# Features of the second half in two of three units, constants loaded first, samples four and first joins five steps later

## What is computed

```python
h = rmsnorm(x, norm_gain) * (1 + scale) + shift          # features: 1024 per token
qa, ka, va, za, qb, fb, ib, zb, ga, gb = split(h @ w_in)   # projections
# branch A: three head groups, windows 128 keys back at distance 1, 4, 16
s = q @ k.T * scale - slope * dist;  m = max(s);  p = exp(s - m);  l = sum(p)
o, lse = p @ v / l, m + log(l)                            # prompt; the sample also reads a cache of keys and values
o_a = sum_g softmax_g(lse_g) * o_g                         # join of the three groups
A = (o_a * silu(za)) @ w_branch_a
B = (rmsnorm(hgrn2(silu(qb), sigmoid(fb), ib)) * silu(zb)) @ w_branch_b
y = x + gate * ((sigmoid(ga) * A + sigmoid(gb) * B) @ w_out)
```

## Time and profile before

| | us |
|---|---|
| median of 3 runs (3123.8 to 3127.46) | 3126.55 |
| the profiled execution: its time | 3124.32 |
| its span, first to last instruction | 3122.5 |
| PE busy of the span | 2919.9 |
| projections, recurrence (`phase_weave`) | about 110 to 2121 |
| attention (`phase_mix`) | about 2121 to 2719 |

### The profile page before, as it was taken

The page is one execution under the profiler, slowest core; times in us unless marked ns, Lnnn a source line. Parts: engine busy times, 40 slices in busy tenths (PEclk is TensorE's granted clock), DMA queues, the critical chain, the costliest instruction groups (busy, mean ns, idle before and its releaser), DMA issues. The chain is left out here.

```text
span 3122.5 us, 47274 instructions
## 1 busy us (share of the span) xinstructions
PE 2919.9 (94%) x18020; PEld 2609.9 (84%) x18020; DVE 1361.6 (44%) x3061; ACT 1085.1 (35%) x2165; POOL 836.7 (27%) x704
## 2 busy tenths in 40 slices
PE   7889999999999899999999999995979889589999
PEld 7778998888888799999999999993656656389999
DVE  2584334566544233343565645422434334433333
ACT  1343213444444333212444444442534434221110
POOL 0242333555422222232555533210011112040000
PEclk9999999999999999999999999997989797799999
DMA  6364432332322432322333232227676776353432
GB/s 195 95 178 137 125 95 77 105 98 92 104 99 88 166 113 94 111 84 88 95 100 102 90 100 94 98 71 263 240 262 224 254 246 212 123 194 109 126 119 86
DMA packets 385264, 417.90 MB, mean 134 GB/s; under 512 B 115600, under 2 KB 296080, under 8 KB 378384
## 3 DMA queue, kind: packets, MB, share of 16 engines
q1 hardware_dynamic: 378128, 406.24, 41.0%
q10 hardware_dynamic: 6912, 8.65, 0.8%
HBM read 284.11 MB, written 130.70 MB: 133 GB/s over the span
## 5 line engine op out<-in xcount | busy, mean ns | idle before, releaser
L667 PE MATMUL weave_bank<-h_high,w_high 128*128 128x352 f32 (+2 forms) x2240 | 819.8, 366 | 15.2 <-issue 11.4
L669 PE MATMUL weave_bank<-h_high,w_low 128*128 128x352 f32 (+2 forms) x2240 | 801.4, 358 | 0.0
L668 PE MATMUL weave_bank<-h_low,w_high 128*128 128x352 f32 (+2 forms) x2240 | 799.1, 357 | 0.0
L944 POOL TENSOR_TENSOR w_low<-weave_w_raw,w_high 128x512 fp32r<-128x512 f32 x284 | 379.9, 1349 | 771.1 <-ACT w_high L815 769.2
L667 PEld LDWEIGHTS weave_bank<-h_high,w_high 128*128 128x128 f32 x2240 | 427.0, 191 | 57.5 <-issue 14.7
L669 PEld LDWEIGHTS weave_bank<-h_high,w_low 128*128 128x128 f32 x2240 | 426.0, 190 | 40.4
L668 PEld LDWEIGHTS weave_bank<-h_low,w_high 128*128 128x128 f32 x2240 | 426.0, 190 | 39.7 <-issue 2.9
L679 PE MATMUL weave_bank<-w_high,h_high 128*128 128x256 f32 x1088 | 310.0, 285 | 0.0
L681 PE MATMUL weave_bank<-w_high,h_low 128*128 128x256 f32 x1088 | 306.7, 282 | 0.0
L680 PE MATMUL weave_bank<-w_low,h_high 128*128 128x256 f32 x1088 | 305.6, 281 | 0.0
L1671 ACT ACTIVATE mix_probs<-mix_scores,mix_o_out 128x256 f32<-128x256 f32 (+1 forms) x384 | 157.0, 454 | 319.2 <-DVE mix_o_out L1754 307.1
(11 more groups left out here) (229 smaller groups left out, 4860.6 us busy)
## 6 DMA issues: line engine op xcount, KB each, us to landing
weave_w_raw<-in_w_qkv SPq DMA_DIRECT2D x144, 256.0 KB, 2.9
mix_kv<-in_kT_c SPq DMA_DIRECT2D x24, 1024.0 KB, 7.6
mix_kv<-in_v_c SPq DMA_DIRECT2D x24, 1024.0 KB, 7.1
tail_gates<-scratch_gates SPq DMA_DIRECT2D x48, 352.0 KB, 3.2
weave_w_raw<-in_w_g SPq DMA_DIRECT2D x64, 256.0 KB, 3.0
weave_w_raw<-in_w_b SPq DMA_DIRECT2D x60, 256.0 KB, 2.8
scratch_sums<-mix_o_out SPq DMA_DIRECT2D x48, 264.0 KB, 6.0
mix_rows<-scratch_sums SPq DMA_DIRECT2D x24, 528.0 KB, 6.8
```

The lines of the kernel that those rows point to most:

```text
L667: pe.matmul(dst, w_high[:, i, k, :], h_high[:, k, tok], start=(k == 0), stop=False)
L668: pe.matmul(dst, w_high[:, i, k, :], h_low[:, k, tok], start=False, stop=False)
L669: mm = pe.matmul(dst, w_low[:, i, k, :], h_high[:, k, tok], start=False, stop=(k == KD - 1))
L944: pool.tensor_tensor(w_part(w_low, p), w_raw[p % RAW][:, :, :], w_part(w_high, p), ALU.subtract).then_inc(w_low_done, 1)
```

## The change

It moves work and adds none.

1. Chunk f of the features starts in unit 2 + 3f // 2 (units 2, 3, 5, 6, 8, 9, ..., 26) and keeps its distances between stages.
2. SP issues the seven constants of the projections first, then x and weight pieces in turn.
3. All parts of the sample in the attention, with their loads, `prepare` and copies, come four steps later (`at` begins with 8 instead of 4).
4. The first half of each join but the last pair's is weighed and turned five steps later (`later`); its `rows` are still loaded in the step `start`.

```diff
+        F_AT = {2 + 3 * f // 2: f for f in range(FT)}
...
-                for p in range(4, 7):
-                    load(p)
-                for f in range(FX):
-                    load_x(f)
                 for dst, src in CONSTANTS:
                     sp.dma_start(dst, dr[src]).then_inc(const_in, 16)
+                load_x(0)
+                load(4)
+                load_x(1)
+                load(5)
+                load(6)
+                for f in range(2, FX):
+                    load_x(f)
                 for U in range(len(STEPS)):
...
-                    if 1 <= U < FT + 1:
-                        feature_sums(U - 1)
+                    if U - 1 in F_AT:
+                        feature_sums(F_AT[U - 1])
...
-                    if 1 <= U < FT + 1:
-                        feature_pairs(U - 1)
-                    if 3 <= U < FT + 3:
-                        feature(U - 3)
+                    if U - 1 in F_AT:
+                        feature_pairs(F_AT[U - 1])
+                    if U - 3 in F_AT:
+                        feature(F_AT[U - 3])
...
-    at = lambda i, k: 4 + SPAN * i + k * SPAN // PARTS
+    at = lambda i, k: 8 + SPAN * i + k * SPAN // PARTS
...
-    turn_at = lambda jp, half: start(jp, half) + (12 if jp < PAIRS - 1 else 6 + 2 * half)
+    later = lambda jp, half: 5 if jp < PAIRS - 1 and half == 0 else 0
+    turn_at = lambda jp, half: start(jp, half) + later(jp, half) + (12 if jp < PAIRS - 1 else 6 + 2 * half)
     J_LOAD = {start(*x): x for x in J_HALVES}
-    J_LEAST = {start(*x) + 2: x for x in J_HALVES}
+    J_LEAST = {start(*x) + later(*x) + 2: x for x in J_HALVES}
```

30 lines of the change are left out of this document (15 added, 15 removed).

## The result

The changed kernel takes 3086.5 us in the median of four runs (3082.0 to 3094.2), the kernel before on the same chip 3125.2 (3122.3 to 3127.5): a ratio of 0.988, with a 95% interval from 0.9858 to 0.9903. Forecast were 3060 and a range from 3038 to 3090. The sign and the range held; of the 66 us that I summed up, 39 came. The profiled execution took 3082.05 us against 3124.32, 42.3 less, and the two profiles tell stage by stage where.

A forecast was written before the change was run, and what follows sets the result against it. PE, busy 94% of the span, bounds the kernel, so only its waits and half-clock work can be won. Gains of 21.4 + 5.0 + 29 + 11 = 66.4 us from 3124.3 give 3057.9, forecast 3060 as median, range 3038 to 3090.

The forecast's parts named there:

- Constants first: Start of projections: DVE starts near 117 instead of 125.10, so PE's first wait of 8.0 us goes entirely.
- Features in two of three units: Projections: DVE's work nearly even with PE's, 18.4 against 17.6 us per three curved units; 6.4 us of waits stay.
- the collision with POOL: Projections: pairs cost 2.7 us when POOL splits weights at the same moment; if all do, 12 us of waits stay.
- the clock's 6.5: Projections: half-clock loss behind PE's waits, four times about 1.7 us, counted in the ceiling of 27.8 us.
- 21.4 forecast: Projections in all: ceiling 27.8 us of waits and clock less 6.4 that stay; bounds 15.8 and 27.8.
- DVE still the bound: Rival, projections: DVE bounds curved units, 12 us stay with two clock dips, 10 us less gain, 3069; chance 0.12.
- Samples four steps later: Attention start: two waits become one for the key cache; four steps of 1.25 us gained, 5.0 us, bounds 3 to 8.
- First joins five steps later: Attention's three joins: five steps fill PE's waits and rows land earlier; 12, 11 and 6 gone, 29 us, bounds 12 to 38.
- the 4.9 of the sum: Second join: the job's loads go 4.9 us earlier, losing a wait of 3.65 us for a part and a step.
- The rule that completion isn't first in, first out: Joins, second case: if transfers don't land in issue order, only the five steps' 18.7 us are won.
- Clock in the attention: Behind the joins: half-clock loss returns, 8 us at the second, 3 at the third, none at the first; 11 us, bounds 0 to 20.
- The rival nearest to the time, 3081: Attention: rows land where they do now, joins give 18.7 us and the clock nothing; 45 us gained in all; chance 0.16.

The follow-up runs named there:

- the four profiles with this attention: Two profiles of the changed kernel, one with its features split, one with POOL writing zeros instead of subtracting; attention 526.1 to 534.2 us.
- four others with the same steps there: Four profiles of other kernels in which nothing was moved at the second join; the 17 us at half clock there are gone.
- the fastest kernel: Changed kernel with two second halves five steps later, last samples three steps earlier, first halves' rows issued two steps earlier: 3056.8 us, 0.9784 of before.
- the kernel with the 44 us: Changed kernel with the next job's loads (3 MB) three steps later, behind the join's rows and key cache: 3083.8 us, 0.9867 of before.
- another: Kernel before with only the constants first and the samples four steps later: 3093.3 us, 0.9903 of before.

## Why the prediction was right, and where it was not

**Constants first: right.** DVE's first instruction was to come near 117 and came at 115.56; the 8.0 us went entirely, and the edit alone brought 9.4 for 9.7.

**Features in two of three units: right in kind, a little short in size.** The waits were to stay behind units 6, 15, 18 and 21. They stand behind 6, 7, 15, 18 and 21, 7.9 us in one execution and 10.0 in the other, against 6.4. The cause was the one that I had as a bound, the collision with POOL, with pairs at 2.7 (1.51 + 1.23 in front of the wait of 2.80), and it is shown by the kernel whose POOL reads nothing. What I undersized is that a feature can collide in two or three of its products (4.2 to 5.2 us), where I had let one collide (3.1).

**The term that failed here** is the clock's 6.5: I let all of it go, and kept 6.4 us of waits in the same sentence. The waits that stayed brought their dips (0.83 at 250). 21.4 forecast, 14.3 in the profile, 17 in most others. The rival "DVE still the bound", 10 us less than the forecast, had both the collision and the dips in it, and for this stage it was the better case.

**Samples four steps later: right at the start, incomplete behind.** One wait for the key cache of some 8 us at step 8 was forecast, and 8.03 is there. PE's two waits of 5.05 and 11.54 were 16.6 us together, so 8.6 went and not 5.0, just over the bound of 8: the four steps ran at the half level, some 2.1 us each as in the earlier trace rows, and not at 1.25. That the same shift puts 2 MB in front of the third join's rows stood in the text; that the 0.5 MB behind them would be the longest wait of all did not (10.18 against 4 to 10, at the end of the bounds).

**First joins five steps later: right in kind and near in size.** First join: 5 left, waiting for the cache and no longer for rows; it was 5.55. Second: none over 2 us; so it was. Third: 6.5 taken, 10.2 measured. The second came out by luck in part: the samples alone took 1.8 us there for the 4.9 of the sum, which with five steps would leave 4.3, and what took the rest isn't shown. 42 us of waits became 17 (with one of 1.3 behind the first), so 25 for the 29 of the sum. A wait moved by 5.7 and another by 4.9 us when 2 MB changed their place in the queue, and in the bursts of the first and third join each transfer landed in the order of issue or within 0.3 us of it. The rule that completion isn't first in, first out (the Trainium skill, page "DMA: Bandwidth & Descriptors", section "Queues, rings and completion order"), which would have made it 18.7, decided nothing here.

**Clock in the attention: wrong.** 11 us forecast, -3 measured (and +4 to -8 by the four profiles with this attention). The step that failed is "with the second wait gone I give its 8 back": the wait went, and the half level did not go with it. Of the 37 us at half behind the second join 31 are left, in two pieces. The 17 us at the join itself have no wait over 0.53 us in front; both profiles of the changed kernel have them (17 and 14), four others with the same steps there don't, and the cause stays open. The 14 us at the turns are what I could have seen: I had looked only at who waits where today, and not at what the moved turns would now lie across. Five steps later they reach from step 70 to step 77 of a round, and from step 75 on DVE works on the second half, its rows and its weights. I followed the moved step through the transfers and not through DVE's own order. The waits are small (3.44, 1.38 and 1.38). Moving the second halves along gave 9 to 11 us, which is of the size of most of the 14 that were missing.

**The sum.** 66.4 forecast for the profiled execution, 42.3 measured: 7 short in the projections; 14 at the attention's clock; 7 in its waits (4 at the joins and 6 for the new ones of the turns, less some 4 that the start gave beyond its 5); and 4 more than forecast in the part behind, which lies within what that part scatters. The split between clock and waits is that of two single profiles. The rival nearest to the time, 3081, was wrong in its reason: the rows did land earlier.

## What to carry to other kernels

When a step is moved to give a transfer time, look on every engine at what the moved instructions now lie across, above all at a wait or at other work in an in-order engine between two of them: moving the second half along with the first was worth as much as a quarter of the whole change. Compare PE's busy time over the same instructions before and after: if the waits shrink and the busy time doesn't, the clock hasn't come back with them. Do it over several profiles: here the same attention scattered by 8 us and its busy time by 12. Count a wait that two edits both cure once, and let a clock dip go only together with the last wait in front of it.

## What the runs showed of the hardware

The granted clock was at its half level for 44 us while PE was busy in all of them; ahead of the fall PE was busy 12.20 of 14 us, with waits of 1.28 and 0.34 us. In the fastest kernel the same place has 20 us at 0.51, PE busy 20.00, behind waits of 6.12 and 1.28. Fewer waits are thus no promise of the full clock: the kernel with the 44 us waited 33.1 us in its attention and was busy 503.3, another waited 61.2 and was busy 476.6.

DVE's product of two operands in SBUF beside a subtraction on POOL took 1.67 to 1.79 us for 0.69 alone, and POOL's own could get longer too (L996 1.61 above, 1.29 elsewhere in the same profile); beside POOL's memset it took 0.69.

Two MB moved in front of or behind a burst shifted a wait by 4.9 and 5.7 us, close to the 6.1 that they weigh at 346 GB/s.
